# First norm's modulation by halves of columns, and four reorderings around the first attention

## The chip, the cores and the metric

One core of one Trainium2 chip runs the kernel. Times are device microseconds of that core. Three runs of the kernel before took 1524.25, 1528.77 and 1528.91 us, median 1528.77.

## The reference, cut to what matters

A two-layer encoder on 256 tokens of width 1024, in float32, batch 1. Every sub-layer reads a normalised stream that is scaled and shifted by rows computed from the conditioning vector c:

```
cond = jax.nn.silu(c)
mod = cond @ ada_w[l] + ada_b[l]                  # (1, 6144): shift, scale, gate of attention, then of the channel mixer
h = rms_norm(x, norm_attn[l]) * (1 + sc_a) + sh_a
```

Layer 0: h @ w_qkv (1024 x 3072), differential attention over 8 heads (two softmax maps a head, RMS norm of queries, keys and outputs per head, a relative bias), @ w_o, a gated residual; the same norm and modulation again, a dense SwiGLU (2816). Then a shared key/value projection, layer 1 with window attention, and eight expert SwiGLUs (3584) of which each token takes two.

## The kernel before, in words

The program is written out by hand for each engine, in an order that is fixed; engines wait for each other on counting semaphores. Tokens stand as two blocks of 128 (index i). A weight unit is 128 x 1024 floats (512 KB). SyncE's queue loads units and pieces of ada_w in the order of `ring_order` (RING) into the 12 slots of WRAW; it waits for the reader of a slot before it loads it again (`slot_read`). For each unit k, ScalarE makes the rounded high part (`hi`, WHI, 6 slots), VectorE the low part (`lo`, WLO), and TensorE does three products for each block and half (`block_products`, 12 matmuls of 512 columns a unit). The normalised input is transposed on TensorE (`ht_transposes`), copied as high part by ScalarE (`ht_his`) and as low part by VectorE (`ht_los`), four of 128 columns at a time. Units 0 to 7 project queries, 8 to 15 keys, 16 to 23 values, 24 to 31 are w_o, 32 to 37 begin the feed-forward.

The rows of the modulation are sums over 8 pieces of ada_w (128 x 1024, piece k holds rows 8p + k): VectorE multiplies a piece by a column of c and adds it to a row of MOD (`early_product`), and TensorE sums that row over the partitions with a matrix of ones, in fp32 (`mm(PS, ones, MOD)`). Two of the 16 pieces of the first scale and shift go straight through TensorE (`EARLY_PE`, `early_piece`). The norm's first use is written out in the VectorE program, lines 1248 to 1279: products, `fold` (gain times 1 + scale), two scaled rows, then the shift added in four halves, which releases the transposes. GpSimd's program (from line 578) clears rows, loads biases and gains (behind `ada_used` 10), stores the table of relative biases, reads it back as tiles after `w_lo` 14, and from line 618 loads the late pieces of ada_w into SHR.

After unit 20 TensorE transposes the normed keys, ScalarE copies them (`transposed(4, ...)`, line 877) behind the high parts of units 24 and 25; logits of heads 0 and 1 follow after unit 21. VectorE's `biased` adds the bias and takes the maximum. `project_by_block` does w_o block by block in the order BLOCK_FIRST: (0,0) to (0,4), (1,0), (1,1), (0,5) to (0,7), (1,2) to (1,7), where (i,k) is block and unit. In it stands `shift_sum`, the sum of the shift row of the feed-forward's norm, which waits for the last early product of VectorE; ScalarE copies it (`mod_rows(MOD0[3], 2, 4)`) before it makes the high part of unit 32 and the root of the next norm. Released by `h_ready` 12, GpSimd clears rows and begins the late transfers.

## Time and profile before

| | us |
|---|---|
| median of three runs | 1528.77 |
| the profiled execution, its own time | 1525.94 |
| its span, first to last instruction | 1524.1 |
| TensorE busy | 1466.6 (96%) |
| VectorE busy | 1292.8 (85%) |
| ScalarE busy | 979.9 (64%) |
| GpSimd busy | 130.7 (9%) |
| HBM traffic | 324 GB/s mean |

Busy time is time with an instruction of the engine running; a share near 100% in a stretch says that the engine was not made to wait there. One fp32 matmul of 512 columns is two records. Start times are from the span's start. In a row of a timeline the bracket gives the idle time of the engine before the instruction, and what ended it. "x7" merges seven instructions of one kind, and the time is that of all.

### The profile page before, as it was taken

Reading aid. Unit: us, or ns where it says so; the run is one execution under the profiler, and the core shown is the slowest. Engines: PE = TensorE matmul, PEld = TensorE weight load, DVE = VectorE, ACT = ScalarE, POOL = GpSimd, SP = SyncE. Lnnn points to the kernel's source line nnn. Section 1 sums busy time; section 2 is a strip of 40 time slices with the busy share of each in tenths; the row PEclk is TensorE's granted clock in tenths of the full one; section 3 lists DMA queues with packets and bytes.
Section 4 is the critical chain, followed back from the end, with each engine's and each line's share of the span. In section 5 each row is a group of like instructions: output and inputs, shape, how many; then the busy total and the mean of one; then the engine's idle time right before and its main releaser. Section 6 shows DMA issues by size and latency. Waiting matters only on the chain.

```text
span 1524.1 us, 22197 instructions
## 1 busy us (share of the span) xinstructions
PE 1466.6 (96%) x6546; PEld 1152.2 (76%) x6546; DVE 1292.8 (85%) x1383; ACT 979.9 (64%) x1249; POOL 130.7 (9%) x143
## 2 busy tenths in 40 slices
PE   6998889999999999999999999999999999999997
PEld 2774667777677678888888888888888888888885
DVE  6888779988776788898898898888889889888896
ACT  3557343444556466777777777677777777777773
POOL 3000122211119000000000000000000000000100
PEclk9999999999999999999999999999999999999999
DMA  9984489998743479999999999999999999999993
GB/s 355 371 294 148 153 296 388 384 369 299 193 152 111 152 252 361 373 374 381 366 364 382 367 360 390 364 356 391 370 361 381 371 363 372 366 360 372 396 394 121
DMA packets 212228, 494.37 MB, mean 324 GB/s; under 512 B 16433, under 2 KB 39185, under 8 KB 212177
## 3 DMA queue, kind: packets, MB, share of 16 engines
q1 hardware_dynamic: 196848, 440.46, 79.6%
q0 software_dynamic: 14528, 51.22, 9.5%
q10 hardware_dynamic: 802, 2.06, 0.4%
q8 instruction: 26, 0.43, 0.1%
q14 instruction: 24, 0.20, 0.0%
HBM read 487.13 MB, written 6.55 MB: 324 GB/s over the span
## 4 chain that ended last, share of the span: by engine, by line
PE 90%; DVE 5%; ACT 2%; DMA 2%; issue 1%; SPq 0%; DVEq 0%; ACTq 0%
PE PS L1694 87%; PE PS L2211 2%; DMA WRAW<-in_ada_w 1%; DVE MOD L1094 1%; DVE WLO L1080 1%; PE PS L1744 1%; PE PS L1817 0%; DVE HT_LO L1153 0%; PE PS L2189 0%; DMA WRAW<-in_a_w_o 0%; DVE X L1236 0%; DVE H L1235 0%; SPq L439 0%; PE PS L1994 0%; DVE ss L1160 0%
## 5 line engine op out<-in xcount | busy, mean ns | idle before, releaser
L1080 DVE TENSOR_TENSOR WLO<-WRAW,WHI 128x1024 fp32r<-128x1024 f32 x790 | 915.7, 1219 | 39.1 <-ACT WHI L697 38.5
L697 ACT ACTIVATE WHI<-WRAW 128x1024 fp32r<-128x1024 f32 x790 | 779.6, 1052 | 90.9 <-PE PS L1694 70.0
L1694 PE MATMUL PS<-WHI,HT_HI 128*128 128x512 f32 x1280 | 516.0, 403 | 9.9 <-DVE HT_LO L1153 6.4
L1694 PE MATMUL PS<-WLO,HT_HI 128*128 128x512 f32 x1280 | 508.0, 397 | 0.0
L1694 PE MATMUL PS<-WHI,HT_LO 128*128 128x512 f32 x1280 | 434.4, 396 | 0.0
L1694 PEld LDWEIGHTS PS<-WHI,HT_HI 128*128 128x128 f32 x1280 | 241.6, 189 | 67.6 <-DVE WLO L1080 7.2
L1694 PEld LDWEIGHTS PS<-WHI,HT_LO 128*128 128x128 f32 x1280 | 241.1, 188 | 58.8
L1694 PEld LDWEIGHTS PS<-WLO,HT_HI 128*128 128x128 f32 x1280 | 241.7, 189 | 55.1 <-issue 0.5
L1694 PE MATMUL PS<-WHI,AT_HI 128*128 128x512 f32 x536 | 216.7, 404 | 3.0 <-DVE AT_LO L1375 1.6
L1694 PE MATMUL PS<-WLO,AT_HI 128*128 128x512 f32 x536 | 211.7, 395 | 0.0
L1694 PE MATMUL PS<-WHI,AT_LO 128*128 128x512 f32 x536 | 211.7, 395 | 0.0
L1022 ACT ACTIVATE AT_HI<-PS 128x512 fp32r<-128x512 f32 x56 | 33.5, 599 | 197.4 <-PE PS L2211 197.4
L1694 PEld LDWEIGHTS PS<-WHI,AT_HI 128*128 128x128 f32 x536 | 100.6, 188 | 30.2 <-issue 2.2
L1694 PEld LDWEIGHTS PS<-WLO,AT_HI 128*128 128x128 f32 x536 | 100.6, 188 | 26.7 <-issue 2.9
L1694 PEld LDWEIGHTS PS<-WHI,AT_LO 128*128 128x128 f32 x536 | 100.6, 188 | 24.5
L1606 DVE TENSOR_TENSOR AT_LO<-PS,AT_HI 128x512 fp32r<-128x512 f32 x56 | 38.8, 692 | 92.7 <-ACT AT_HI L1022 92.7
L1105 DVE SCALAR_TENSOR_TENSOR MOD<-SHR,condT,MOD 128x1024 f32<-128x1024 f32 x64 | 82.0, 1281 | 4.2 <-DMA SHR<-in_ada_w 1.5
L665 POOL DMA_DIRECT2D y_rows<-MOD x7 | 4.0, 572 | 792.7 <-DVE MOD L1583 792.7
L907 ACT ACTIVATE AT_HI<-PS 128x512 fp32r<-128x512 f32 x11 | 6.6, 599 | 65.6 <-PE PS L1994 65.6
L1094 DVE SCALAR_TENSOR_TENSOR MOD<-WRAW,condT,MOD 128x1024 f32<-128x1024 f32 x32 | 41.0, 1281 | 6.1 <-DMA WRAW<-in_ada_w 5.5
L1694 PE MATMUL PS<-MOD,CST 128*128 128x512 f32 x64 | 34.8, 656 | 10.9 <-DVE MOD L1094 6.4
L1018 ACT ACTIVATE MOD<-PS 128x512 f32<-128x512 f32 x56 | 33.5, 599 | 15.3 <-PE PS L1694 15.3
(222 smaller groups left out, 860.5 us busy)
## 6 DMA issues: line engine op xcount, KB each, us to landing
WRAW<-in_moe_w_in SPq DMA_DIRECT2D x448, 512.0 KB, 6.4
WRAW<-in_moe_w_out SPq DMA_DIRECT2D x224, 512.0 KB, 5.5
WRAW<-in_ada_w SPq DMA_DIRECT2D x48, 512.0 KB, 8.8
SHR<-in_ada_w POOLq DMA_DIRECT2D x48, 512.0 KB, 6.6
WRAW<-in_ffn_w_in SPq DMA_DIRECT2D x88, 256.0 KB, 7.9
WRAW<-in_a_w_qkv SPq DMA_DIRECT2D x24, 512.0 KB, 12.9
WRAW<-in_ffn_w_out SPq DMA_DIRECT2D x22, 512.0 KB, 6.3
SHR<-in_kv_ada_w POOLq DMA_DIRECT2D x16, 512.0 KB, 6.8
```

The source lines that it names most:

```text
L665: pool.dma_start(Y_ROWS.ap()[e * P:(e + 1) * P, :], Y).then_inc(y_stored, 16)
L697: nc.scalar.activation(WHI[:, u.split(k), :], WRAW[:, u.raw(k), :], ACT.Copy).then_inc(w_hi, 1)
L907: nc.scalar.activation(AT_HI[:, :], PS[:, 2, :], ACT.Copy).then_inc(at_hi, 1)
L1018: nc.scalar.activation(ESIL, PS[:, 0, :], ACT.Silu).then_inc(e_silu, 1)
L1022: nc.scalar.activation(AT_HI[:, :], PS[:, 2, :], ACT.Copy).then_inc(e_at_hi, 1)
L1080: V_.tensor_tensor(WLO[:, u.split(k), :], WRAW[:, u.raw(k), :], f32(WHI[:, u.split(k), :]), ALU.subtract).then_inc(w_lo, 1)
L1094: V_.scalar_tensor_tensor(row, piece, condT[:, k:k + 1], row, ALU.mult, ALU.add).then_inc(ada_used, 1)
L1105: V_.scalar_tensor_tensor(row, ADA[:, k % ADA_SLOTS, :], condT[:, k:k + 1], row, ALU.mult, ALU.add).then_inc(ada_used, 1)
L1606: V_.tensor_tensor(AT_LO[:, :], PS[:, 2, :], f32(AT_HI[:, :]), ALU.subtract).then_inc(e_at, 1)
L1694: return nc.tensor.matmul(out, a, b, start=start, stop=stop)
L1744: last = nc.tensor.transpose(PS[:, 2 * i + half, k * P:(k + 1) * P], src[:, i, c:c + P], ident)
L2211: last = nc.tensor.transpose(PS[:, 2, c * P:(c + 1) * P], EACT[:, c * P:(c + 1) * P], ident)
```

## The change

The first scale and shift are loaded in pieces of two k by 512 columns, in the order scale half 0, shift half 0, units 0 to 3, scale half 1, unit 4, shift half 1, unit 5 and on. VectorE does the eight scale products of each half (`scale_products`), TensorE all eight shift products of each half (`first_shift`). The norm is scaled and shifted half by half. TensorE transposes half 0, projects units 0 to 2, sums the scale of half 1, projects unit 3, does the shift products of half 1 and six filling matmuls, transposes half 1 and goes on with unit 4. Two filling matmuls stay before the first transposes where there were four. The identity-times-iota work of VectorE moves behind lo 5; the exponential of lambda on ScalarE moves behind hi 2 with another table load; GpSimd's bias and gain loads wait for all 16 scale products.

Further: the key copies come before hi 24 and 25, and the table load between; hi 26 and 27 move behind the first two pairs of exponentials; lo 24 with its product stands between the first two `biased`, and lo 25, 26, 27 behind them; `shift_sum` moves from after (0,5) to after (1,2); the low parts of block 1 of the feed-forward's input come before lo 36. The diff, with declarations and removed lines of the old norm left out:

```diff
@@ -80,7 +80,11 @@
...
-EARLY_PE = ((0, 3), (0, 7))
+SCALE_A = [[("scale_a", half, pair) for pair in range(KT // 2)] for half in range(2)]
+SHIFT_A = [[("shift_a", half, pair) for pair in range(KT // 2)] for half in range(2)]
+EARLY_PE = SHIFT_A[0] + SHIFT_A[1]
+EARLY_DVE = SCALE_A[0] + SCALE_A[1]
+A_UNITS = 4
 SCALE_F0 = 4
@@ -90,8 +94,12 @@
...
-    order = [(1, k) for k in range(KT)] + [(0, k) for k in range(KT)]
+    order = SCALE_A[0] + SHIFT_A[0]
     for n in range(3 * KT):
+        if n == A_UNITS:
+            order += SCALE_A[1]
+        if n == A_UNITS + 1:
+            order += SHIFT_A[1]
         if n in GATE_AT:
@@ -425,6 +435,8 @@
...
                     sp.wait_ge(ada_pe, PE_PIECES.index(what) + 1)
+                elif what in EARLY_DVE:
+                    sp.wait_ge(scale_used, 2 * EARLY_DVE.index(what) + 2)
                 elif what in DVE_PIECES:
@@ -440,9 +452,18 @@
...
-            for c in (1, 0):
-                for k in range(KT):
-                    load_piece((c, k), t["ada_w"][0], c * D)
+            def load_half(pieces, col):
+                for what in pieces:
+                    place, half, k = PLACE[what], what[1], 2 * what[2]
+                    slot_read(place - RAW_SLOTS)
+                    c = col + half * 512
+                    sp.dma_start(WRAW[:, place % RAW_SLOTS, :].rearrange("p (k n) -> p k n", k=2),
+                                 t["ada_w"][0].rearrange("(p k) n -> p k n", p=P)[:, k:k + 2, c:c + 512]
+                                 ).then_inc(w_landed[place % RAW_SLOTS], 16)
+            load_half(SCALE_A[0], D)
+            load_half(SHIFT_A[0], 0)
@@ -459,6 +480,10 @@
...
                     n = g * KT + k
+                    if n == A_UNITS:
+                        load_half(SCALE_A[1], D)
+                    if n == A_UNITS + 1:
+                        load_half(SHIFT_A[1], 0)
                     if n in GATE_AT:
@@ -577,7 +602,7 @@
...
             pool.wait_ge(mod_cleared, 2)
-            pool.wait_ge(ada_used, 10)
+            pool.wait_ge(scale_used, 2 * KT)
             pool.dma_start(MOD[0:1, 2:5, :], t["ada_b"][0:1, 2 * D:5 * D].rearrange("o (c n) -> o c n", c=3)
@@ -797,6 +822,7 @@
...
                 if a == "A":
+                    hi(Units(U_QKV), 26, 27)
                     act.wait_ge(w_used, U_WO)
@@ -847,14 +873,18 @@
...
                 squares(X[:, i, :], i)
-            act.wait_ge(sq_read, 1)
-            nc.scalar.activation(neglam[:, 0:2], neglam[:, 0:2], ACT.Exp).then_inc(sq_ready, 1)
             act.wait_ge(cst_landed, 16)
...
             u = Units(U_QKV)
-            hi(u, 0, 1)
-            ht_his(0, BY_HALF)
+            hi(u, 0)
+            ht_his(0, BY_HALF[:2])
+            hi(u, 1, 2)
+            act.wait_ge(sq_read, 1)
+            nc.scalar.activation(neglam[:, 0:2], neglam[:, 0:2], ACT.Exp).then_inc(sq_ready, 1)
+            load_table(ACT.Sqrt)
+            hi(u, 3, 4)
+            ht_his(0, BY_HALF[2:])
@@ -873,10 +903,9 @@
...
             transposed(0, lambda n: Q[:, n // 2, (n % 2) * 512:(n % 2) * 512 + 512], 0, range(0, 4), qkt_psum)
+            transposed(4, lambda n: K[:, n // 2, (n % 2) * 512:(n % 2) * 512 + 512], 1, range(0, 4), qkt_psum)
+            load_table(ACT.Exp)
             hi(u, 24, 25)
-            transposed(4, lambda n: K[:, n // 2, (n % 2) * 512:(n % 2) * 512 + 512], 1, range(0, 4), qkt_psum)
-            hi(u, 26, 27)
-            load_table(ACT.Exp)
             attention("A")
@@ -1088,11 +1117,43 @@
...
                     dve.wait_ge(ada_used, n)
-                if c < 2 and k == 0:
-                    V_.tensor_scalar(row, piece, condT[:, k:k + 1], None, ALU.mult).then_inc(ada_used, 1)
-                else:
-                    V_.scalar_tensor_tensor(row, piece, condT[:, k:k + 1], row, ALU.mult, ALU.add
-                                            ).then_inc(ada_used, 1)
+                V_.scalar_tensor_tensor(row, piece, condT[:, k:k + 1], row, ALU.mult, ALU.add
+                                        ).then_inc(ada_used, 1)
+            def scale_products(half, pairs):
+                row = MOD[:, MOD0[1], half * 512:half * 512 + 512]
+                for pair_of_k in pairs:
+                    place = PLACE[SCALE_A[half][pair_of_k]]
+                    dve.wait_ge(w_landed[place % RAW_SLOTS], landed_at(place))
+                    for c in range(2):
+                        k = 2 * pair_of_k + c
+                        piece = WRAW[:, place % RAW_SLOTS, c * 512:c * 512 + 512]
+                        if k:
+                            dve.wait_ge(scale_used, half * KT + k)
+                            V_.scalar_tensor_tensor(row, piece, condT[:, k:k + 1], row, ALU.mult, ALU.add
+                                                    ).then_inc(scale_used, 1)
+                        else:
+                            V_.tensor_scalar(row, piece, condT[:, k:k + 1], None, ALU.mult).then_inc(scale_used, 1)
+            def first_scaled(half, bank):
+                cols = slice(half * 512, half * 512 + 512)
+                dve.wait_ge(mod_sum, half + 1)
+                dve.wait_ge(gain_first, 16)
+                V_.scalar_tensor_tensor(MOD[:, MOD0[1], cols], PS[:, bank, :], 1.0, GB[:, cols],
+                                        ALU.add, ALU.mult).then_inc((fold_half, gain_used)[half], 1)
+                dve.wait_ge((fold_half, gain_used)[half], 1)
+                for i in range(TB):
+                    chain(V_.scalar_tensor_tensor(H[:, i, cols], X[:, i, cols], nx[:, i, 1:2],
+                                                  MOD[:, MOD0[1], cols], ALU.mult, ALU.mult))
+            def first_shifted(half, bank):
+                cols = slice(half * 512, half * 512 + 512)
+                dve.wait_ge(ada_pe, len(SHIFT_A[0]) * (half + 1))
+                for i in range(TB):
+                    V_.tensor_tensor(H[:, i, cols], H[:, i, cols], PS[:, bank, :], ALU.add).then_inc(h_ready, 1)
@@ -1245,44 +1306,36 @@
...
             dve.wait_ge(cond_ready, 1)
-            for n in range(0, 4):
-                early_product(n)
+            scale_products(0, range(KT // 2))
+            await_root()
+            chain(V_.reciprocal(nx[:, :, 1:2], nx[:, :, 1:2]))
+            dve.wait_ge(toep_mm, NBIAS // TOEP_HEADS)
+            first_scaled(0, 6)
             dve.wait_ge(lam_landed, 16)
...
             V_.tensor_reduce(neglam[:, 0:2], lv[:, :, 0, :], axis=AX, op=ALU.add).then_inc(sq_read, 1)
-            for n in range(4, KT):
-                early_product(n)
-            for n in range(KT, KT + 2):
-                early_product(n)
-            await_root()
-            chain(V_.reciprocal(nx[:, :, 1:2], nx[:, :, 1:2]))
-            dve.wait_ge(mod_sum, 2)
-            fold(MOD0[1], pair(6), 1)
-            dve.wait_ge(cst_landed, 16)
+            first_shifted(0, 4)
+            u = Units(U_QKV)
+            lo(u, 0)
+            ht_los(0, BY_HALF[:2])
+            lo(u, 1)
+            scale_products(1, range(0, 1))
+            lo(u, 2)
+            scale_products(1, range(1, 3))
+            lo(u, 3)
+            scale_products(1, range(3, 4))
+            lo(u, 4)
+            first_scaled(1, 0)
+            first_shifted(1, 2)
+            ht_los(0, BY_HALF[2:])
+            lo(u, 5)
             chain(V_.tensor_tensor(MOD[:, 5, 0:P], ident, iota, ALU.mult))
...
             V_.tensor_scalar(tokid[:, 1, :], tokf[:, :].broadcast_to([P, 2]), float(P), None, ALU.add).then_inc(ey_ready, 1)
...
             dve.wait_ge(modb_landed, 32)
-            rest = iter(range(2 * KT - len(EARLY_PE), DVE_EARLY))
+            rest = iter(range(DVE_EARLY))
@@ -1290,8 +1343,7 @@
...
-            lo(u, 2, 3)
-            for k in range(4, 14):
+            for k in range(A_UNITS + 2, 14):
                 lo_and_products(k, k in GATE_AT)
@@ -1318,13 +1370,12 @@
...
                 lo_and_products(k, (k in GATE_AT) + (k in SCALE_AT))
-            lo_and_products(24, 0)
-            lo_and_products(25, 1)
             dve.wait_ge(bias_landed, 16 * TOEP_HEADS)
...
             biased("A", 0)
+            lo_and_products(24, 1)
             biased("A", 1)
-            lo(u, 26, 27)
+            lo(u, 25, 26, 27)
             attention("A")
@@ -1362,9 +1413,8 @@
...
             norm(1, H, MOD[:, MOD0[3], :])
-            lo(u, 36)
             ht_los(2, BLOCKS[2:])
-            lo(u, 37)
+            lo(u, 36, 37)
@@ -1875,31 +1925,30 @@
...
             pe.wait_ge(modb_first, 16)
-            for c, bank in ((1, 6), (0, 4)):
-                for half in range(2):
-                    mm(PS[:, bank + half, :], ones, MOD[:, 7 + c, half * 512:half * 512 + 512], True, False)
-            pe.wait_ge(ada_used, KT)
-            for half in range(2):
-                mm(PS[:, 6 + half, :], ones, MOD[:, MOD0[1], half * 512:half * 512 + 512], False, True
-                   ).then_inc(mod_sum, 1)
-            def early_piece(c, k):
-                place = PLACE[c, k]
-                pe.wait_ge(w_landed[place % RAW_SLOTS], landed_at(place))
-                last = (c, k) == EARLY_PE[-1]
-                for half in range(2):
-                    done = mm(PS[:, 4 + half, :], condT[:, k:k + 1].broadcast_to([P, P]),
-                              WRAW[:, place % RAW_SLOTS, half * 512:half * 512 + 512], False, last)
-                done.then_inc(ada_pe, 1)
-            early_piece(*EARLY_PE[0])
-            for _ in range(4):
+            def first_sums(half, scale_bank, shift_bank):
+                cols = slice(half * 512, half * 512 + 512)
+                mm(PS[:, scale_bank, :], ones, MOD[:, 8, cols], True, False)
+                mm(PS[:, shift_bank, :], ones, MOD[:, 7, cols], True, False)
+                pe.wait_ge(scale_used, KT * (half + 1))
+                mm(PS[:, scale_bank, :], ones, MOD[:, MOD0[1], cols], False, True).then_inc(mod_sum, 1)
+            def first_shift(half, bank):
+                for what in SHIFT_A[half]:
+                    place = PLACE[what]
+                    pe.wait_ge(w_landed[place % RAW_SLOTS], landed_at(place))
+                    for c in range(2):
+                        k = 2 * what[2] + c
+                        last = mm(PS[:, bank, :], condT[:, k:k + 1].broadcast_to([P, P]),
+                                  WRAW[:, place % RAW_SLOTS, c * 512:c * 512 + 512], False, k == KT - 1)
+                    last.then_inc(ada_pe, 1)
+            first_sums(0, 6, 4)
+            first_shift(0, 4)
+            for _ in range(2):
                 mm(PS[:, 0, :], ones, CST[:, 0:512])
-            pe.wait_ge(ada_used, 2 * KT - len(EARLY_PE))
-            for half in range(2):
-                mm(PS[:, 4 + half, :], ones, MOD[:, MOD0[0], half * 512:half * 512 + 512], False, False)
-            for piece in EARLY_PE[1:]:
-                early_piece(*piece)
@@ -1909,8 +1958,15 @@
...
             u = Units(U_QKV)
-            ht_transposes(H, [(i, half, h_ready, 2 * half + i + 1) for half in range(2) for i in range(TB)])
-            project(u, 0, 4, splits=0)
+            ht_transposes(H, [(i, 0, h_ready, i + 1) for i in range(TB)])
+            project(u, 0, 4, range(0, A_UNITS - 1), splits=0)
+            first_sums(1, 0, 2)
+            project(u, 0, 4, range(A_UNITS - 1, A_UNITS), splits=0)
+            first_shift(1, 2)
+            for _ in range(6):
+                mm(PS[:, 1, :], HT_HI[:, 0, 0:P], HT_HI[:, 0:2, :])
+            ht_transposes(H, [(i, 1, h_ready, TB + i + 1) for i in range(TB)])
+            project(u, 0, 4, range(A_UNITS, KT), splits=0)
             project(u, KT, 0)
@@ -1944,7 +2000,7 @@
...
                 (0, 2): second_rows,
-                (0, 5): shift_sum,
+                (1, 2): shift_sum,
                 (1, 6): lambda: ht_transposes(H, h_parts(2, BLOCKS[:2]))})
```

## Rows read from the trace of the kernel before

**Rows 1.** busy time by stage: start:end, length, busy us by engine, clock, DMA share, GB/s

```profile
40.40:85.60 45.20, 45.17 (x193) 36.31 (x194) 34.68 (x37) 20.29 (x23) 2.61 (x4) 1.00 1.03 343
...
110.00:120.00 10.00, 8.45 (x34) 6.06 (x32) 8.25 (x18) 6.17 (x15) 0.00 (x0) 0.83 0.62 233
...
240.00:260.00 20.00, 20.00 (x86) 15.54 (x85) 19.47 (x19) 8.22 (x11) 4.24 (x8) 1.00 1.05 391
...
600.00:1500.00 900.00, 900.00 (x3996) 726.63 (x3995) 800.95 (x763) 669.59 (x734) 15.40 (x16) 1.00 1.00 370
```

**Rows 2.** timeline of TensorE: start us, us, instruction, idle before and its releaser

```profile
15.00 5.50 PE L1694 MATMUL PS<-MOD,CST 128*128 128x512 f32 x8 [4.48 <-DMA MOD<-in_ada_b]
...
27.84 3.60 PE L1694 MATMUL PS<-CST 128*128 128x512 f32 x8
...
36.81 2.45 PE L1744 MATMUL PS<-CST,H 128*128 128x128 f32 x16 [0.85 <-DVE H L1278]
...
40.43 0.47 PE L1694 MATMUL PS<-WHI,HT_HI 128*128 128x512 f32 x1 [1.17 <-DVE HT_LO L1153]
...
109.37 0.71 PE L1694 MATMUL PS<-MOD,Q 64*128 64x128 f32 x8 [2.95 <-ACT MOD L764]
...
172.70 3.44 PE L1694 MATMUL PS<-MOD,CST 128*128 128x512 f32 x4 [3.74 <-DVE MOD L1094]
...
199.96 0.77 PE L1694 MATMUL PS<-WHI,HT_HI 128*128 128x512 f32 x1 [3.58 <-DVE HT_LO L1153]
```

**Rows 3.** timeline of VectorE

```profile
12.88 1.28 DVE L1094 SCALAR_TENSOR_TENSOR MOD<-WRAW,condT,MOD 128x1024 f32<-128x1024 f32 x1 [0.81 <-DMA WRAW<-in_ada_w]
...
36.07 2.48 DVE L1278 TENSOR_TENSOR H<-H,PS 128x512 f32<-128x512 f32 x4 [1.35 <-PE PS L1694]
...
42.00 8.03 DVE L1080 TENSOR_TENSOR WLO<-WRAW,WHI 128x1024 fp32r<-128x1024 f32 x7
...
86.63 1.22 DVE L1160 TENSOR_REDUCE ss<-W 128x16 f32<-128x1024 f32 x1 [5.97 <-ACT W L863]
...
115.08 0.42 DVE L1186 TENSOR_TENSOR MOD<-PS,SHR 128x256 f32<-128x256 f32 x1 [0.84 <-PE PS L1694]
...
118.50 0.42 DVE L1186 TENSOR_TENSOR MOD<-PS,SHR 128x256 f32<-128x256 f32 x1 [0.63 <-PE PS L1694]
...
169.89 2.67 DVE L1094 SCALAR_TENSOR_TENSOR MOD<-WRAW,condT,MOD 128x1024 f32<-128x1024 f32 x2
...
183.21 1.42 DVE L1142 SCALAR_TENSOR_TENSOR H<-H,nx,MOD 128x512 f32<-128x512 f32 x2
...
199.12 1.28 DVE L1153 TENSOR_TENSOR HT_LO<-PS,HT_HI 128x512 fp32r<-128x512 f32 x2
...
209.85 1.28 DVE L1105 SCALAR_TENSOR_TENSOR MOD<-SHR,condT,MOD 128x1024 f32<-128x1024 f32 x1 [0.49 <-DMA SHR<-in_kv_ada_w]
```

**Rows 4.** timeline of ScalarE

```profile
32.72 1.06 ACT L697 ACTIVATE WHI<-WRAW 128x1024 fp32r<-128x1024 f32 x1 [13.34 <-DMA WRAW<-in_a_w_qkv]
...
37.50 2.39 ACT L756 ACTIVATE HT_HI<-PS 128x512 fp32r<-128x512 f32 x4 [2.32 <-PE PS L1744]
...
104.64 1.06 ACT L697 ACTIVATE WHI<-WRAW 128x1024 fp32r<-128x1024 f32 x1 [6.20 <-DMA WRAW<-in_a_w_o]
...
106.91 2.41 ACT L764 ACTIVATE MOD<-PS,gcol 128x512 f32<-128x512 f32 x4
...
176.24 1.03 ACT L741 ACTIVATE MOD<-PS 128x1024 f32<-128x1024 f32 x1 [7.53 <-PE PS L1694]
...
195.81 1.20 ACT L756 ACTIVATE HT_HI<-PS 128x512 fp32r<-128x512 f32 x2 [0.92 <-PE PS L1744]
```

**Rows 5.** timeline of GpSimd

```profile
25.43 0.66 POOL L581 DMA_DIRECT2D MOD<-in_ada_b  x1 [21.14 <-DVE MOD L1094]
...
87.57 0.96 POOL L600 MEMSET SHR<- 64x1024 f32 x1 [18.79 <-DMA SHR<-toep_rows]
...
195.72 2.67 POOL L622 MEMSET MOD<- 128x3072 f32 x1 [30.07 <-DVE H L1142]
```

More of the change, by code:

```diff
@@ L109 @@
 POOL_PIECES = [("gate_f", k) for k in range(KT)]
-DVE_PIECES = [what for what in RING if isinstance(what, tuple) and what not in PE_PIECES and what not in POOL_PIECES]
+DVE_PIECES = [what for what in RING if isinstance(what, tuple) and what not in PE_PIECES + POOL_PIECES + EARLY_DVE]
 DVE_EARLY = len(DVE_PIECES)
@@ L287, in trunk @@
         ada_used = sem("ada_used")
+        scale_used = sem("scale_used")
         pool_used = sem("pool_used")
@@ L291, in trunk @@
         mod_ready = sem("mod_ready")
+        fold_half = sem("fold_half")
         scale_psum = sem("scale_psum")
@@ L864, in block_squares @@
                 root(ss[:, i, 0:width // 64], 64)
-            hi(u, *range(2, 14))
+            hi(u, *range(5, 14))
             act.wait_ge(w_used, U_QKV + KT)
@@ L1266, in _ @@
             V_.tensor_scalar(tokid[:, 1, :], tokf[:, :].broadcast_to([P, 2]), float(P), None, ALU.add).then_inc(ey_ready, 1)
-            for n in range(KT + 2, 2 * KT - len(EARLY_PE)):
-                early_product(n)
-            dve.wait_ge(toep_mm, NBIAS // TOEP_HEADS)
-            dve.wait_ge(gain_used, 1)
-            for i in range(TB):
-                chain(V_.scalar_tensor_tensor(H[:, i, :], X[:, i, :], nx[:, i, 1:2], MOD[:, MOD0[1], :],
-                                              ALU.mult, ALU.mult))
-            dve.wait_ge(ada_pe, len(EARLY_PE))
-            for half in range(2):
-                cols = slice(half * 512, half * 512 + 512)
-                for i in range(TB):
-                    V_.tensor_tensor(H[:, i, cols], H[:, i, cols], PS[:, 4 + half, :], ALU.add
-                                     ).then_inc(h_ready, 1)
-            u = Units(U_QKV)
-            lo(u, 0)
-            ht_los(0, BY_HALF)
-            lo(u, 1)
             dve.wait_ge(modb_landed, 32)
-            rest = iter(range(2 * KT - len(EARLY_PE), DVE_EARLY))
+            rest = iter(range(DVE_EARLY))
             def lo_and_products(k, n):
@@ L1895, in _ @@
-            early_piece(*EARLY_PE[0])
-            for _ in range(4):
-                mm(PS[:, 0, :], ones, CST[:, 0:512])
-            pe.wait_ge(ada_used, 2 * KT - len(EARLY_PE))
-            for half in range(2):
-                mm(PS[:, 4 + half, :], ones, MOD[:, MOD0[0], half * 512:half * 512 + 512], False, False)
-            for piece in EARLY_PE[1:]:
-                early_piece(*piece)
+            def first_sums(half, scale_bank, shift_bank):
[4 more added lines that the diff above has]
+                mm(PS[:, scale_bank, :], ones, MOD[:, MOD0[1], cols], False, True).then_inc(mod_sum, 1)
```

## The prediction

> **What bounds the kernel now.** I read the busy times by stage first. In the expert stage, more than half of the span, TensorE is busy 900.00 of 900.00 us, and in the dense feed-forward 20.00 of 20.00 [rows 1]. Nothing in those stages is changed, so whatever the first 200 us win or lose reaches the end unaltered, unless the entry of the feed-forward takes it back. Then I read TensorE's own timeline of the first 200 us [rows 2]. The first projection starts at 40.43 us and runs 16 units without a break in 45.17 us [rows 1], 2.82 us a unit. Then three waits stand out: 2.95 us at 109.37 for ScalarE's key copies, 3.74 us at 172.70 for VectorE's last shift products, 3.58 us at 199.96 for the low part of the feed-forward's input. Then VectorE's timeline [rows 3], which shows who is behind each of them, ScalarE's [rows 4] and GpSimd's [rows 5].
>
> **The start, part by part.** Before, TensorE begins its modulation work at 15.00, held 4.48 us by the transfer of the bias row. Four fp32 products of 512 columns take 5.50 us there; four later ones without a gap take 3.60 us, 0.90 each [rows 2]. So two of the first four ran at the low rate, (5.50 - 1.80) / 2 = 1.85 us each. The change moves the six shift products that VectorE did (6 x 1.28 us) to TensorE and cuts all work in halves. TensorE's chain, with the same start at 15.00:
> - two bias sums and one scale sum of half 0: 3.70 + 0.90, to 19.6. The scale products are ready: the fourth transfer landed at 12.88 [rows 3], its two half products (0.71 each, half of the 1.42 of two 512-column ones [rows 3]) end near 14.3.
> - eight shift products on TensorE: 7.2, to 26.8. Their transfers are there: the 17th landed at 32.72 [rows 4], so from the fourth they come (32.72 - 12.88) / 13 = 1.53 us apart, the eighth near 19.0.
> - two filling matmuls 1.8, to 28.6; VectorE adds the shift in the meantime (4 adds in 2.48 [rows 3], 0.62 each). Then one block of transposes 0.61 (16 in 2.45 [rows 2]), its high part 0.60 [rows 4] and its low part 0.6, and 0.2 to start: unit 0 begins at 30.6, 9.8 us earlier than now.
> - units 0 to 2: 8.5, to 39.1. The sums of half 1: 2.7, to 41.8. The last wait there is for the scale products of half 1: the 16th transfer lands near 31.2, and VectorE has lo 0 to 2, three pairs of products, lo 3 and the fourth pair to do (products 1.4 a pair, a low part 1.15: seven in 8.03 [rows 3]), which ends near 40.4, before the 40.9 at which TensorE wants it.
> - unit 3 to 44.6, eight shift products 7.2 to 51.8, six filling matmuls of 0.235 to 53.2, transposes, high and low part and start again 2.0: unit 4 begins at 55.2.
> Before, unit 4 began at 40.43 + 4 x 2.82 = 51.7. The early start is real, but TensorE is the engine that pays for it: 24 fp32 products instead of 16, of 0.9 us, and a second transpose latency. **The split costs 3.5 us.** The bounds: 1 us, if the exposed pieces overlap; 6 us, if the array falls to the low rate in one of the two gaps of about 1 us (the gap of 1.17 before 40.43 did not do that [rows 2], the one of 2.95 did: in 110 to 120 the granted clock is 0.83 [rows 1]).
>
> What moves beside it: GpSimd's bias and gain transfers now wait for all 16 scale products (40.4) where they waited for the tenth (25.43 [rows 5]), so the table's store follows 15 us later too. Its bias tiles are gated by lo 13 anyway and land near 87.57 + 3.5 [rows 5], needed at 110: nothing. In SyncE's queue unit 4's load waits for the first shift product on TensorE (21.4) and the shift pieces of half 1 for the next three and lo 0. At 21.4 the eight transfers before them are still on their way until 31.2, so the DMA does not run dry: nothing. The exponential of lambda and a second table load go into ScalarE's queue before hi 3, which is wanted at 37: nothing.
>
> **Key copies and low parts before attention.** The key projection now ends 3.5 later, and VectorE's key norm with it: 86.63 becomes 90.1. From 86.63 to 114.2 VectorE has no gap, then waits 0.84 before 115.08 [rows 3]. So the same work ends at 117.8. Lo 26 now waits for a high part that ScalarE makes after the second pair of exponentials, 0.7: attention begins at VectorE at about 118.4, +3.3. The copies no longer stand behind a weight that lands at 104.64 [rows 4]: copies at 105.9 to 108.3, unit 21 ends at 109.7, so TensorE's 2.95 us wait goes and with it the low rate, (1 - 0.83) x 10 = 1.7 us. These 4.6 us are not paid out: VectorE is the later one. They only let it run without waiting. Before, it waited 0.84 and then 0.63 at 118.50, with four more such gaps (0.43, 0.17, 0.44, 0.38) up to 129 [rows 3]. The five sum to 2.05, so of +3.3 **+1.3 us** is left at the end of attention. Between -1.5 (TensorE sets the pace, and starts the last unit earlier) and +3.3 (the gaps are latency and stay).
>
> **The shift sum.** Before, it stands after (0,5): TensorE waits until 172.70, then needs 3.44 us for two products at the low rate [rows 2], and (0,6), (0,7) and (1,2) follow. ScalarE's hi 32 waits for (1,2), which ends at 176.1 + 3 x 1.41 = 180.4, and the norm's root stands behind it. After the change (in before's time, without the +1.3): (0,5) ends at 168.96, (0,6), (0,7), (1,2) at 173.2; the products end at 172.56 [rows 3], so no wait; two sums at 0.9 end at 175.0. The copy of the shift row, 1.03 us [rows 4], runs to 176.1, and hi 32 finds its slot free: 4.3 us earlier. Block 0's residual (173.7, after the fold) is ready for it. The root, the norm of block 0, two low parts, block 1's residual and norm all follow in VectorE's order: **-4.3 us**. Bounds: -5.3 (the residual alone) and -1.1 (the copy alone, 176.24 to 175.1).
>
> **Low part of block 1 before lo 36.** VectorE does the first input low part at 199.12, behind lo 36, which itself waited for ScalarE; ScalarE makes the two high parts from 195.81, 0.6 each [rows 4]. So the first low part can follow at 196.4 and TensorE start 2.7 us sooner, and block 1's four units run at the full rate (another 1.6). But 8 us after that VectorE must do a late product whose transfer GpSimd issues only after its memset at 195.72, itself released by the norm of block 1 [rows 5]; at 209.85 VectorE waited for the second of them [rows 3], and from there it is full: 19.47 of 20 us at 240 [rows 1]. The transfers move by the 4.3 only, and the low parts of the next weights stand behind those products. I take **0**; bound -4.3, if the transfers land sooner or the products had slack.
>
> **Sum.** +1.3 - 4.3 = -3.0 us. The profiled execution took 1525.94 (span 1524.1 and 1.84 around it): 1522.9. The three timed runs are 1524.25, 1528.77 and 1528.91; the median lies 2.8 above the profiled one. I set the sum against the mean of all four, 1527.0: **1524.0 us**.
>
> **Rivals.**
> 1. The bias row lands sooner. TensorE's last product before the modulation ends at 10.5, so the 4.48 us wait at 15.00 is all for an 8 KB transfer on ScalarE's queue [rows 2]. The pieces on SyncE's queue now come in rows of 2 KB instead of 4 KB, at two rows to a partition. If the engines share by row, ScalarE's queue gets more, TensorE starts up to 3.3 us sooner (the scale products at 14.3 and the shift pieces 1.53 apart allow no more), the split costs near 0, attention ends 1 to 2 us sooner than in my sum: about -5, 1522.0. For it: both queues are full then. Against: scale pieces would come later by as much. 
> 2. The gaps of attention are latency. Then the whole +3.3 stays: 3.3 - 4.3 = -1.0, 1526.0. For it: in the second half of attention TensorE and VectorE alternate almost without slack.
> 3. Slower: the pieces of half rows move at half the rate. A piece then costs some 2.7 us instead of about 1.5, the last shift piece of half 1 lands near 60 where TensorE wants it by 50, and unit 3 waits for the scale pieces: 8.6 us more: 3.5 + 8.6 - 2.0 (the gaps) - 4.3 = +5.8, 1532.8. It decides from the point at which a piece takes over 2 us. Against: the feed-forward's weights come in rows of 1 KB, and at 240 to 260 the core moves 391 GB/s [rows 1].
>
> **Chances.** Forecast 0.45, rival 1 0.25, rival 2 0.18, rival 3 0.12. Range 1519 to 1530: rival 1 with half of the last bound below, rival 2 and the scatter of the runs (4.7 us) above. A measurement of this kernel can tell 0.3%, 4.6 us, from no change. My likeliest case lies at that edge against the median: faster by more in all of rival 1 and a little under half of the forecast, 0.25 + 0.21 = 0.46; slower is rival 3 and 0.01, 0.13; the rest, 0.41, is no change.
>
> **What would show it.** Right: the first unit near 30.6 and the fifth near 55.2; K norm at 90; no wait for the key copies and a granted clock near 1.00 in 110 to 120; attention about 1.3 us later; the shift sum without a wait, hi 32 right behind the copy; TensorE into block 1 some 6 us earlier, and a new wait for low parts 5 us later. Wrong: a fifth unit before 52 (then rival 1), VectorE's gaps in attention as before (rival 2), any wait of VectorE for a half piece after 31 (rival 3), or a feed-forward that starts its third pair of weights over 6 us earlier.

## The result, and the profile after

The changed kernel took 1522.19 us (median of 15 runs, 1515.31 to 1525.61), the kernel before 1527.84 (15 runs): a ratio of 0.9962, 95% interval 0.9951 to 0.9973. That is 0.38% faster, 5.8 us by the ratio and 5.65 by the medians, clear of noise. The profiled execution took 1522.19 with a span of 1520.4, against 1525.94 and 1524.1: 3.75 less. One execution of e8 (2067.68 us, mean granted clock 0.656) and one of e10 (2713.99, 0.831) stand far from all others and are in no median or ratio below.

TensorE's timeline after answers to [rows 2] (the line of `mm` is L1744 now):

```profile
12.28 3.37 PE L1744 MATMUL PS<-MOD,CST 128*128 128x512 f32 x4 [1.96 <-DMA CST<-in_cst]
...
18.10 1.67 PE L1744 MATMUL PS<-MOD,CST 128*128 128x512 f32 x2 [2.46 <-DVE MOD L1134]
...
19.57 8.22 PE L1744 MATMUL PS<-WRAW,condT 128*128 128x512 f32 x16
...
31.45 0.47 PE L1744 MATMUL PS<-WHI,HT_HI 128*128 128x512 f32 x1 [1.07 <-DVE HT_LO L1214]
...
45.30 7.03 PE L1744 MATMUL PS<-WRAW,condT 128*128 128x512 f32 x16
...
55.66 0.47 PE L1744 MATMUL PS<-WHI,HT_HI 128*128 128x512 f32 x1 [1.07 <-DVE HT_LO L1214]
...
208.67 0.50 PE L1744 MATMUL PS<-WHI,HT_HI 128*128 128x512 f32 x1 [1.93 <-DVE WLO L1109]
```

The modulation starts at 12.28 and not at 15.00, and what it waited for last there is the table of constants (`in_cst`), no longer the bias row. But its scale sum waits until 18.10. The eight shift products of a half take 8.22 and 7.03 us. The first unit starts 9.0 us earlier than before, the fifth at 55.66, where before it started at 51.7. No wait for key copies, and none before the shift sum, is left; a new one stands at 208.67, for the low part of unit 38.

VectorE's timeline, beside [rows 3]:

```profile
16.51 1.54 DVE L1134 SCALAR_TENSOR_TENSOR MOD<-WRAW,condT,MOD 128x512 f32<-128x512 f32 x2 [2.60 <-DMA WRAW<-in_ada_w]
...
90.59 1.22 DVE L1221 TENSOR_REDUCE ss<-W 128x16 f32<-128x1024 f32 x1 [4.55 <-ACT W L893]
...
119.12 0.42 DVE L1247 TENSOR_TENSOR MOD<-PS,SHR 128x256 f32<-128x256 f32 x1
...
129.55 0.42 DVE L1247 TENSOR_TENSOR MOD<-PS,SHR 128x256 f32<-128x256 f32 x1 [0.45 <-PE PS L1744]
...
131.52 0.69 DVE L1247 TENSOR_TENSOR S<-PS,SHR 128x512 f32<-128x512 f32 x1 [0.38 <-PE PS L1744]
...
204.41 1.28 DVE L1166 SCALAR_TENSOR_TENSOR MOD<-SHR,condT,MOD 128x1024 f32<-128x1024 f32 x1 [2.83 <-DMA SHR<-in_kv_ada_w]
```

The fourth pair of scale products comes 3.6 us later than the fourth piece did (12.88). The key norm is 4.0 us late, the first maximum of attention (the row at 119.12, before 115.08) also 4.0. In attention two of its waits stay (129.55 and 131.52). At 204.41 VectorE waits 2.83 us for the first late piece.

ScalarE's timeline and, in the second fence, GpSimd's, beside [rows 4] and [rows 5]:

```profile
106.30 2.43 ACT L789 ACTIVATE MOD<-PS,gcol 128x512 f32<-128x512 f32 x4 [2.76 <-PE PS L1805]
...
151.07 1.28 ACT L743 ACT_TABLE_LOAD   x1
...
177.49 1.03 ACT L766 ACTIVATE MOD<-PS 128x1024 f32<-128x1024 f32 x1 [6.26 <-PE PS L1744]
...
178.41 1.05 ACT L722 ACTIVATE WHI<-WRAW 128x1024 fp32r<-128x1024 f32 x1
...
193.40 1.20 ACT L781 ACTIVATE HT_HI<-PS 128x512 fp32r<-128x512 f32 x2 [0.91 <-PE PS L1794]
```

```profile
193.31 2.67 POOL L647 MEMSET MOD<- 128x3072 f32 x1 [25.15 <-DVE H L1203]
```

The key copies wait for TensorE's transposes alone. The table load at 151.07 marks the end of attention; before it was at 148.55, so attention ends 2.5 late. The shift row's copy is 1.2 us late, the high part of unit 32 follows it at once, the high part of block 1 comes 2.4 early (195.81 before), and GpSimd's memset as well (195.72).

By stage, with the granted clock third from the right, beside [rows 1]:

```profile
110.00:120.00 10.00, 7.86 (x42) 5.48 (x40) 9.07 (x13) 7.57 (x16) 0.00 (x0) 1.00 0.92 370
...
120.00:155.00 35.00, 28.24 (x139) 15.00 (x140) 31.74 (x81) 27.82 (x94) 0.57 (x1) 0.95 0.46 155
...
210.00:220.00 10.00, 10.00 (x38) 7.96 (x38) 9.79 (x10) 3.90 (x5) 2.64 (x5) 0.84 1.04 389
...
600.00:1500.00 900.00, 900.00 (x3996) 726.67 (x3995) 801.15 (x757) 669.37 (x735) 16.74 (x16) 1.00 1.00 369
```

### The profile page after: what moved, and what is told of

Same layout as the page of the kernel before. It is cut to its first block, busy times and chain, and to the rows that moved or that the text cites. A ratio compares the mean times of both kernels' runs of the same rounds, so it can differ in the third digit from the quotient of the medians.

```text
span 1520.4 us, 22242 instructions
## 1 busy us (share of the span) xinstructions
PE 1473.4 (97%) x6568; PEld 1155.9 (76%) x6568; DVE 1287.7 (85%) x1388; ACT 980.4 (64%) x1251; POOL 131.8 (9%) x143
## 4 chain that ended last, share of the span: by engine, by line
PE 90%; DVE 6%; ACT 1%; DMA 1%; issue 1%; POOL 0%; SPq 0%; DVEq 0%; ACTq 0%
PE PS L1744 86%; PE PS L2267 2%; DVE WLO L1109 1%; DMA WRAW<-in_ada_w 1%; DVE MOD L1120 1%; PE PS L1794 1%; DMA SHR<-in_kv_ada_w 1%; DVE HT_LO L1214 0%; PE PS L1867 0%; PE PS L2245 0%; DVE H L1203 0%; DVE sm L1251 0%; DVE X L1297 0%; DVE H L1296 0%; PE PS L2050 0%
## 5 line engine op out<-in xcount | busy, mean ns | idle before, releaser
L1744 PE MATMUL PS<-WHI,HT_HI 128*128 128x512 f32 x1280 | 515.2, 402 | 10.3 <-DVE HT_LO L1214 4.9
L1744 PE MATMUL PS<-WLO,HT_HI 128*128 128x512 f32 x1280 | 507.5, 396 | 0.0
L1744 PE MATMUL PS<-WHI,HT_LO 128*128 128x512 f32 x1280 | 434.0, 396 | 0.0
L1744 PEld LDWEIGHTS PS<-WHI,HT_HI 128*128 128x128 f32 x1280 | 241.2, 188 | 68.2 <-issue 8.6
L1744 PEld LDWEIGHTS PS<-WHI,HT_LO 128*128 128x128 f32 x1280 | 240.8, 188 | 58.6
L1744 PEld LDWEIGHTS PS<-WLO,HT_HI 128*128 128x128 f32 x1280 | 241.1, 188 | 55.2 <-issue 0.7
L1744 PE MATMUL PS<-WHI,AT_HI 128*128 128x512 f32 x536 | 216.7, 404 | 3.0 <-DVE AT_LO L1425 1.6
L1744 PE MATMUL PS<-WLO,AT_HI 128*128 128x512 f32 x536 | 211.7, 395 | 0.0
L1744 PE MATMUL PS<-WHI,AT_LO 128*128 128x512 f32 x536 | 211.7, 395 | 0.0
L1744 PEld LDWEIGHTS PS<-WHI,AT_HI 128*128 128x128 f32 x536 | 100.6, 188 | 30.2 <-issue 2.2
L1744 PEld LDWEIGHTS PS<-WLO,AT_HI 128*128 128x128 f32 x536 | 100.6, 188 | 26.7 <-issue 2.9
L1744 PEld LDWEIGHTS PS<-WHI,AT_LO 128*128 128x128 f32 x536 | 100.6, 188 | 24.5
L781 ACT ACTIVATE HT_HI<-PS 128x512 fp32r<-128x512 f32 x24 | 13.5, 596 | 45.7 <-PE PS L1794 45.4
L1652 DVE TENSOR_TENSOR MOD<-MOD,PS 128x512 f32<-128x512 f32 x56 | 38.2, 683 | 0.1
```

The source lines that it names most:

```text
L781: nc.scalar.activation(HT_HI[:, 4 * half:4 * half + 4, i * P:(i + 1) * P], PS[:, 2 * i + half, :].rearrange("p (k s) -> p k s", k=4), ACT. ...
L1652: V_.tensor_tensor(EACT, ESIL, PS[:, 1, :], ALU.mult).then_inc(e_act, 1)
L1744: return nc.tensor.matmul(out, a, b, start=start, stop=stop)
```

## Experiments

All times are medians, ratios are to the kernel before as it ran beside each experiment, with 95% intervals. The changed kernel did not run beside the experiments, and the median of the kernel before was 1527.13 beside e1 to e4, 1526.49 beside e5 to e10 and 1526.15 beside e11 to e13, for 1527.84 beside the changed kernel. A difference between two changed kernels is given by the medians; where the ratios say something else, both stand. "End of attention" and "end of feed-forward" are ScalarE's table loads there, in the profile of each kernel (before: 148.55 and 393.18; changed: 151.07 and 390.10).

**e1, the four reorderings on the old first norm.** The first norm's part of the diff is taken back, the rest stays.

> The kernel before with the four reorderings (key copies and low parts, shift sum, low part of block 1) but its own first norm, whole rows. Theory (the split costs TensorE 3.5 us, the reorderings bring the gain): first projection at 40.4 and key norm at 86.6 as before, attention ends 1 us sooner than before, shift sum without a wait, in all 5 to 6 us under the kernel before, 2 to 3 us under the changed kernel. Rival (the split pays by its early start, the reorderings need it): no faster than the kernel before minus 3, and slower than the changed kernel.

1517.35 us, ratio 0.9931 (0.9916 to 0.9947): 9.8 us under the kernel before, 4.8 under the changed one. The first unit starts at 41.08, the key norm at 87.27, attention ends at 147.76, the feed-forward at 386.92. The direction is the theory's, the gain is larger than the 5 to 6 us it said. In the profiles 6.3 us of it are there at the end of the feed-forward, and another 5.1 come behind it, in a stretch that nothing changed and that this execution ran at a higher clock (below); the median keeps 3.5 of these. The rival falls: the interval lies wholly under that of the changed kernel.

**e2, the split alone.** The reverse: key copies, low parts, shift sum and block 1 in the old order.

> The changed kernel with all four reorderings undone: the split of the first norm alone. Theory: key norm 4 us later than in the kernel before, the 3 us wait for the key copies and the 3.7 us wait before the shift sum still there, 3 to 4 us slower than the kernel before. Rival (the split pays): 1 to 3 us faster than the kernel before.

1529.43 us, ratio 1.0012 (1.0000 to 1.0023): 1.8 us slower than before by the ratio, 2.3 by the medians, at the edge of noise. The key norm is 4.9 late (91.49), attention ends at 153.76, 5.2 late, and TensorE's two waits are there (3.30 and 3.74 us). The direction is the theory's, the size in the runs is half to two thirds of it. The split does not pay. Its price on top of the reorderings, 4.8 us from e1 to the changed kernel, is larger; at the end of attention, ahead of the stretches whose clock varies (below), it is 3.3 there.

**e3, the shift sum back.**

```diff
-                (1, 2): shift_sum,
+                (0, 5): shift_sum,
```

> The changed kernel with the shift sum back after (0,5). Theory: TensorE waits some 3.7 us before it and does its two products at the low rate, the next norm is 4.3 us later; 4 to 5 us slower than the changed kernel, about as slow as the kernel before or 1 us slower. Rival (the entry of the feed-forward hides it, since TensorE waits there anyway): under 1.5 us slower than the changed kernel.

1526.46 us, ratio 0.9997 (0.9985 to 1.0009): 4.3 us slower than the changed kernel by the medians, 5.3 by the ratios, and clear of its interval, as the theory had it. TensorE waits 3.75 us for the sum, and its two products take another 3.75 (its timeline, first fence). By the windows (second fence) it is busy 4.25 of the 8 us from 172, and the clock is low behind them:

```profile
179.23 3.75 PE L1744 MATMUL PS<-MOD,CST 128*128 128x512 f32 x4 [3.75 <-DVE MOD L1120]
```

```profile
172.00:180.00 8.00, 4.25 (x16) 2.95 (x16) 5.85 (x5) 2.12 (x2) 0.18 (x1) 0.91 0.00 0
...
180.00:190.00 10.00, 10.00 (x30) 6.78 (x29) 3.12 (x4) 2.59 (x3) 0.00 (x0) 0.73 0.83 249
```

**e4, the key copies and low parts back.** ScalarE's part of the edit, shortened; the move of hi 26 and 27 out of attention and of VectorE's low parts 24 to 27 goes with it.

```diff
-            transposed(4, ...)      # key copies
-            load_table(ACT.Exp)
             hi(u, 24, 25)
+            transposed(4, ...)
+            hi(u, 26, 27)
+            load_table(ACT.Exp)
```

> The changed kernel with the key copies and the high and low parts of units 24 to 27 in the old order. Theory: the 2.95 us wait of TensorE and the low rate in the value projection are back, attention ends 1 to 2 us later than in the changed kernel, which passes through: 1 to 2 us slower than the changed kernel. Rival (TensorE's wait is paid in full): 4 to 5 us slower. Second rival (VectorE is late in either order): no difference.

1523.37 us, ratio 0.9973 (0.9962 to 0.9984): 1.2 us slower than the changed kernel by the medians, 1.7 by the ratios; the two intervals overlap, so the runs alone do not show it. Attention ends at 152.99, 1.9 later, though its key norm came 1.8 sooner (88.82): from key norm to the end of attention it takes 64.2 us for 60.5. TensorE's wait for the key copies is back, 4.07 us at 112.67, and so is the low rate, by e4's windows:

```profile
110.00:120.00 10.00, 7.33 (x27) 5.54 (x28) 7.03 (x11) 7.54 (x17) 0.00 (x0) 0.66 0.78 314
```

The clock of 0.66 is 3.4 us of full speed lost in these ten. So a wait of 4.07 us and 3.4 us of lost speed on TensorE cost 3.7 us in attention, not 7.5: VectorE is the later engine, and only what it is made to wait shows.

**e5, lo 36 ahead of block 1's low part again.**

```diff
+            lo(u, 36)
             ht_los(2, BLOCKS[2:])
-            lo(u, 36, 37)
+            lo(u, 37)
```

> The changed kernel with lo 36 again ahead of the low part of block 1. Theory: block 1 of the feed-forward starts 2 to 3 us later, but TensorE's wait of 1.93 us for lo 38 behind the late product, and the low rate after it, go or move ahead of block 1; within 1 us of the changed kernel. Rival (the reordering is paid): 2 to 3 us slower than the changed kernel.

1521.59 us, ratio 0.9969 (0.9955 to 0.9984): no slower than the changed kernel by the medians, 1.1 us slower by the ratios, no difference clear of noise. Block 1 starts at 199.72 behind a wait of 3.58 us, and the wait of 1.93 us for lo 38 is gone, as the theory had it. From the table load behind block 1's norm to the end of the feed-forward it takes 199.95 us for 199.11. This reordering is worth 1 us at most here; with the late pieces early it was not taken apart.

**e8, the late pieces early, on e1.** GpSimd clears the key/value rows, loads their bias and issues the first four late pieces before it waits for the norm of block 1; VectorE waits for that bias alone.

```diff
+            pool.dma_start(MOD[0:1, 7:9, :], ...kv_ada_b...).then_inc(modb_kv, 16)
+            ada_load(0, t["kv_ada_w"], 0, range(ADA_SLOTS))
             pool.wait_ge(h_ready, 12)
             pool.memset(MOD[:, 2:5, :], 0.0).then_inc(mod_cleared, 1)
```

> The four reorderings on the old first norm (as e1), and GpSimd issues the key/value bias and the first four late pieces before it waits for the norm of block 1, not after its memset. Theory (the entry of the feed-forward is tied to these transfers): no wait of VectorE for them, TensorE's 2 us wait for lo 38 under 0.7 us, no low rate behind it, 2 to 3.5 us faster than e1. Rival (VectorE's own work is the tie): under 1 us.

1514.48 us, ratio 0.9918 (0.9897 to 0.9939): 2.9 us under e1 by the medians, 2.0 by the ratios, the fastest kernel of all. **e13** is the same kernel again:

> The same kernel as e8 (reorderings on the old first norm, late pieces issued early), for its profile beside more runs. Theory: median 1514 to 1516, no wait of VectorE for the late pieces, no low rate between 200 and 220.

1515.56 us, ratio 0.9921 (0.9900 to 0.9943), 1.8 us under e1. The intervals of e8, e13 and e1 overlap; the profiles show the gain more plainly: from the table load behind block 1's norm to the end of the feed-forward e1 takes 199.25 us (187.67 to 386.92), e13 195.40. VectorE's first two late products run without a wait (e13's timeline of VectorE, first fence), and so does TensorE from 200 to 220 (its windows, second fence):

```profile
200.67 2.67 DVE L1108 SCALAR_TENSOR_TENSOR MOD<-SHR,condT,MOD 128x1024 f32<-128x1024 f32 x2
...
203.26 1.22 DVE L1083 TENSOR_TENSOR WLO<-WRAW,WHI 128x1024 fp32r<-128x1024 f32 x1
```

```profile
200.00:210.00 10.00, 10.00 (x47) 8.10 (x46) 9.56 (x10) 4.69 (x6) 2.11 (x4) 1.00 0.87 279
...
210.00:220.00 10.00, 10.00 (x45) 8.05 (x44) 9.79 (x9) 4.39 (x5) 2.11 (x4) 1.00 1.00 393
```

So the entry was tied to these transfers. The changed kernel has the same waits (2.83 us on VectorE, 1.93 on TensorE), so it leaves this gain lying; the edit was not run on it.

**e9, and the low parts of the first step before its late products.** In `f_step(0)` the four late products follow both low parts.

> As e8, and the first step of the feed-forward does its two low parts before its four late products. Theory: the rest of TensorE's wait goes too, 0 to 1 us faster than e8. Rival: the products are then late for the next steps and VectorE is full there, 0 to 2 us slower than e8.

1515.09 us, ratio 0.9924 (0.9898 to 0.9951): no difference from e8 and e13 clear of noise. Once the pieces are there, this order does not matter as far as these runs can tell.

**e10, no filling matmuls.** The two before the first and the six before the second transposes are left out.

> The changed kernel without the two filling matmuls before the first transposes and the six before the second. Theory (they end as the shift is added, and cost nothing by themselves): fifth unit within 1 us of 55.66; at equal clock 0 to 1 us faster than the changed kernel; if the array falls to the low rate in the gaps of then 2.5 us, 1 to 3 us slower.

1524.61 us, ratio 0.9981 (0.9962 to 0.9999): 2.4 us slower than the changed kernel by the medians, 2.9 by the ratios, with intervals that overlap, although the fifth unit starts 2.8 us earlier, as e10's timeline of TensorE shows (units 0 and 4):

```profile
28.93 0.47 PE L1744 MATMUL PS<-WHI,HT_HI 128*128 128x512 f32 x1 [1.17 <-DVE HT_LO L1214]
...
52.82 0.47 PE L1744 MATMUL PS<-WHI,HT_HI 128*128 128x512 f32 x1 [0.90 <-DVE HT_LO L1214]
```

The expectation put the fifth unit within 1 us of 55.66, so it missed, but most of the 2.8 us is not the filling: the first shift products began 0.9 us sooner (18.69 for 19.57) and took 7.03 us for 8.22. Beside e4, whose first products also took 7.03, the filling costs 0.4 us from their start to unit 0 (10.24 for 10.68); from unit 0 to unit 4 it costs 0.3 (23.89 for 24.21). The array did not fall to the low rate in the gaps that they had filled, the clock being 1.00 up to 110. It fell in attention and behind it, and attention ended at 150.86, only 0.2 earlier than in the changed kernel. By e10's windows:

```profile
120.00:155.00 35.00, 29.24 (x130) 15.77 (x131) 29.41 (x74) 26.58 (x89) 0.57 (x1) 0.84 0.46 155
...
155.00:172.00 17.00, 15.90 (x64) 11.68 (x64) 10.41 (x13) 5.98 (x10) 4.46 (x3) 0.84 0.16 54
```

Whether that follows from the earlier start or is the chance of an execution (e3 and e5 show such stretches too) stays open; these executions scatter from 1518.0 to 1528.0.

**e11, half of the shift products of half 1.** TensorE does only the odd k of half 1, so that half of the shift row lacks four of its eight terms.

```diff
-                    for c in range(2):
+                    for c in range(half, 2):
```

> The changed kernel with four of the eight shift products of half 1 left out on TensorE (their part of the shift is missing). Theory (in the start TensorE's own products are the chain): fifth unit 3.5 us earlier than 55.66, so near 52.1, key norm 3.5 us earlier; total 1 to 3 us faster than the changed kernel. Rival (the pieces' landing or VectorE's scaling is the chain): fifth unit within 1 us of 55.66.

1517.64 us, ratio 0.9934 (0.9908 to 0.9960): 4.6 us under the changed kernel, more than the 1 to 3 expected. Units 0 and 4 in e11's timeline of TensorE:

```profile
29.30 0.47 PE L1744 MATMUL PS<-WHI,HT_HI 128*128 128x512 f32 x1 [1.07 <-DVE HT_LO L1214]
...
50.08 0.47 PE L1744 MATMUL PS<-WHI,HT_HI 128*128 128x512 f32 x1 [1.07 <-DVE HT_LO L1214]
```

From the first unit to the fifth 20.78 us pass, and 24.21 or 24.22 in each of the five profiles that do all of it (the changed kernel, e2 to e5): 3.43 for four products, 0.86 each, one for one. TensorE's products are the chain there. The fifth unit comes 5.6 us earlier and so does the key norm (85.01), where 3.5 was expected: the other 2.2 us lie before the first unit, where nothing was left out. That start scatters from 29.3 to 32.4 among the kernels with the split and its filling, with the end of the scale products and the rate of the first shift products (7.03 us in e4 and e11, 8.22 in the changed kernel, 9.16 in e2).

**e12, rows of 2 KB.** Each of the first 16 pieces comes as two transfers of half the columns, in the kernel before.

> The kernel before with each of its first 16 pieces loaded as two transfers of half the columns, so in rows of 2 KB; all else as before. Theory (ScalarE's queue gets a larger share against shorter rows): bias row there by 12.5 instead of 15.0, the fourth scale piece ready at 15 to 16.5 instead of 12.88; first projection within 1 us of 40.43, total within 2 us of the kernel before. Rival (the order of the pieces, not the rows): both within 0.5 us of the kernel before.

1530.76 us, ratio 1.0020 (1.0002 to 1.0037): 3.1 us slower than the kernel before by the ratio, 4.6 by the medians. The timelines of e12, first TensorE's (two groups of the sums), then VectorE's:

```profile
13.03 5.99 PE L1704 MATMUL PS<-MOD,CST 128*128 128x512 f32 x8 [2.85 <-DMA MOD<-in_ada_b]
...
24.06 3.78 PE L1704 MATMUL PS<-MOD,CST 128*128 128x512 f32 x4 [5.04 <-DVE MOD L1104]
```

```profile
15.34 2.70 DVE L1104 SCALAR_TENSOR_TENSOR MOD<-WRAW,condT,MOD 128x1024 f32<-128x1024 f32 x2 [3.72 <-DMA WRAW<-in_ada_w]
```

The bias row is there at 13.03. The products of the third and fourth scale pieces run from 15.34, where the third alone was at 10.78 and the fourth at 12.88, so the third came 4.6 us later. The scale sum at 24.06 waited 5.04 us and runs at the low rate. So the bias row comes sooner and the pieces later without any change in their order. This edit halves the rows and doubles the number of transfers; the changed kernel halves the rows and keeps the number, and its fourth piece too came late (16.51 for 12.88). What both share is the row of 2 KB. The first unit starts at 43.62, 3.2 late: more than the 1 us that the theory allowed, and the total is beyond its 2 us as well.

## Why the prediction was right, step by step

The forecast was 1524.0, faster by 3.0 against the mean of four executions, 1527.0; 1522.19 lies in the range, and the pair of profiles differs by 3.75. The runs differ by 5.8, nearly twice the sum, so the steps below account for the pair of profiles and for about half of the median's gain.

- **Start.** Right in sum, by two errors that cancel. I kept TensorE's start at 15.00 and the scale products ready at 14.3; they were 12.28 and 18.0, and the scale sum ended at 19.57 for 19.6. That these two met is luck. The first half is rival 1 as described, and the second is the "against" of it: scale pieces later by as much. The wait of 2.46 us for them was not in the working, and the first eight shift products then took 8.22 us for 7.2. The start of unit 0 was 31.45 for 30.6, that of unit 4 55.66 for 55.2, so the split cost 4.0 at the key norm for 3.5.
- **Attention.** The mechanism was right, the term mis-sized: +1.3 forecast, +2.5 measured (151.07 against 148.55). VectorE began 0.7 later than worked out, and of its five gaps the last two stayed as they were (0.45 and 0.38 at 129.55 and 131.52, before 0.44 and 0.38): 0.8 of the 2.05 us that the working took as gained. Rival 2 is partly true. e4 puts the worth of this reordering at 1.2 to 1.7 us in the runs, within noise, and the stretch from key norm to the end of attention is 61.9 us before, 60.5 in e1 and in the changed kernel.
- **Shift sum.** -4.3 forecast. From the end of attention to hi 32 it is 31.92 before (180.47 less 148.55) and 27.34 after: -4.6. e3 gives 4.3 to 5.3 in the runs. Right.
- **Block 1's low part.** Zero, right by e5 within 1 us, and for the reason given: block 1 starts at 194.87 on TensorE for 199.96, 5.1 sooner, and then TensorE waits 1.93 us for lo 38 behind the late product, and runs low after it (clock 0.84 in 210 to 220). e8 removes the tie and gains 2 to 3 in the runs.
- **Sum at the end of the feed-forward**: 393.18 to 390.10, -3.1, for -3.0 forecast.
- **The rest of the measured 5.8** is not in these steps. Between the end of the feed-forward and the entry of the experts nothing differs in the program, yet this stretch takes 133.5 us in e1's profile and 138.3 in the changed kernel's (138.6 in the kernel before's, 134.5 in e5's, 137.0 to 138.5 in those of e2 to e4 and e9 to e13). The table loads that bound it stand at 390.10 and 528.36, in e1 at 386.92 and 520.39. The clock differs, here by the windows of the changed kernel and then of e1:

```profile
420.00:440.00 20.00, 20.00 (x85) 16.29 (x84) 10.98 (x18) 9.63 (x14) 0.00 (x0) 0.88 0.53 158
...
500.00:520.00 20.00, 16.88 (x81) 12.94 (x80) 16.18 (x20) 8.97 (x14) 1.09 (x2) 0.92 0.37 129
...
520.00:540.00 20.00, 19.58 (x105) 14.74 (x104) 15.13 (x40) 11.66 (x15) 0.00 (x0) 0.91 0.37 120
```

```profile
420.00:440.00 20.00, 20.00 (x96) 16.36 (x95) 12.51 (x21) 10.04 (x15) 0.00 (x0) 1.00 0.46 144
...
500.00:520.00 20.00, 16.70 (x93) 12.10 (x91) 15.65 (x25) 11.69 (x18) 1.08 (x2) 1.00 0.42 143
...
520.00:540.00 20.00, 18.35 (x103) 15.32 (x103) 18.08 (x37) 12.04 (x14) 0.00 (x0) 1.00 0.55 180
```

A pause of TensorE stands in both at the same place, 3.23 us ahead of 419.13 in the changed kernel and 3.22 ahead of 415.95 in e1. The clock is low behind the one and stays at 1.00 behind the other, so the pause alone does not decide it.

In the runs of the changed kernel, the six with a mean granted clock of 0.993 and more took 1517.8 us on average, the nine others 1523.5. Of the kernel before, the 71 executions beside the experiments have their clock on record, and 10 of them reach 0.993. At one and the same mean clock, 0.991, the kernel before took 1526.2 us (11 executions) and the changed kernel 1523.5 (6): 2.7 apart, close to the 3.0 of the sum. So about half of the 5.8 is the steps above, and the other half goes with the clock, which is high in 6 of 15 executions instead of 10 of 71. Whether the change brings that, by what it shifts or by the pauses it takes away, or 15 executions are too few, is not shown.

Rival 3 did not occur: VectorE waits for no half piece after 31.

## What to carry to other kernels

Before an early start is bought by halving a stage, add up the engine that must do the extra work: here TensorE got eight more fp32 products of 0.9 us in its own chain, and 9 us of earlier start became 4 us of delay. A bundle of edits should be taken apart even when it wins: four plain reorderings (one of them worth 1 us at most, by e5) gave 9.8 us, and the part that names the change took 4.8 of them back. When an engine arrives earlier at a stage, look who issues the next transfers and what releases that queue; four transfers issued before a wait instead of behind it gave another 2 to 3 us (e8; 1.8 in e13). And where a median moves by more than the stages add up to, compare executions at one granted clock before the rest is explained.

## What was not expected of the hardware

Halving the rows of one queue moved the transfers of the other. With rows of 2 KB for 4 KB on SyncE's queue, the 8 KB bias row on ScalarE's was there at 13.03 us in e12 instead of 15.00 (15.05 in e1, which keeps the long rows). In e12 the third piece on SyncE's queue came 4.6 us later, and in the changed kernel the fourth 3.6 us later. And code that is the same instruction by instruction took 133.5 us at a granted clock of 1.00 and 138.3 where it was 0.88 to 0.95 in four windows of 20 us, behind a pause of TensorE of the same 3.2 us in both.
